# Attention over both heads of a pair at once, with the values held as the stationary operand

## The chip, the cores and the metric

One core of a Trainium2 chip runs the whole program. The metric is the device time of one execution in microseconds (us). Before the change the median of three runs is 4628.94 us (4620.43 to 4631.04). The execution that the profiler recorded took 4612.46 us, of which the profile's span is 4611.2 us.

## The reference

Two transformer blocks of depth 2 run one after the other, in float32, on 512 tokens of width 1024 (the first block has 256 context tokens beside them). Three of their four mixers' layers contain attention with heads of 64 features:

```
# block 1, both layers: 8 query heads, 2 key/value heads, each shared by 4 query heads
k_all = concat([kc, kx]); v_all = concat([vc, vx])          # 256 + 512 = 768 keys
s = einsum('bkgqd,bksd->bkgqs', q, k) * HEAD_DIM ** -0.5
p = softmax(s);  out = einsum('bkgqs,bksd->bkgqd', p, v)
# layer 0 also computes the 256 context queries against the 256 context keys
# block 2, layer 0: 8 heads with keys and values of their own, 512 tokens; every earlier block
# of 256 is selected, so it is causal attention
```

Queries and keys get an RMS norm and an axial rotation in block 1, a partial rotation in block 2. The rest, which the change does not touch, is projections, a Fourier mixer, a gated linear scan (hgrn), feed-forward layers, a short convolution and a linear recurrence (lru).

## The kernel before

Activations lie by features: 128 features on the partitions, tokens along the free dimension. One such chunk of 128 query features is a **pair** of heads, so there are four pairs, c = 0 to 3. Attention runs in three stages: `at0` (layer 0 of block 1), `at1` (layer 1) and `mo` (block 2). Each engine has its own program, written out by hand in the functions `te_` (TensorE), `ac_` (ScalarE), `ve_` (VectorE) and `gp_` (GpSimd); they meet only at semaphores (`wait_ge`; `A.up`, `V.up`, `T.up`, `G.up` raise them). `wait_bank(k)` makes TensorE wait for whoever last read bank k of PSUM; `bank(k, ...)` names that reader. Each engine works strictly in its own program's order.

**A step** is one tile of 128 queries against one head (`attend_steps`, L813). A tile is (first query, first key, number of keys, mask). `at0` has four tiles of 768 keys and two of 256 in each pair, `at1` four of 768, `mo` tiles of 128, 256, 384 and 512 keys with a causal mask on the last 128. Keys are stored once for each head, with the other head's 64 rows zeroed (`KK`, L1100, by a multiplication with the head mask `HM` on VectorE; `KZ`, L1744, the same on GpSimd), so that the full 128 rows of queries can be contracted. A step is:

- scores: queries stationary, masked keys moving, into banks 2k and 2k+1 with k = step mod 2 (L834);
- VectorE: maximum (L952), times minus the scale (L954); ScalarE: exponential with the row sum (L905);
- TensorE transposes the probabilities by blocks of 128 keys into banks 4 and 5 (L848); ScalarE copies bank 4 (L915), VectorE bank 5 (L963), and VectorE takes the reciprocal of the sum (L968);
- values: the transposed probabilities stationary, 128 columns of V moving (64 of them are of use), result by queries in bank 6 (L862);
- VectorE scales 64 columns by the reciprocal (L980); after the second head the 128 by 128 result is transposed back (L870) and ScalarE copies it into `U` (L919).

All programs are staggered two steps deep (loops at L873, L921, L983): scores of step x+2, transposes of x+1, values of x. Scores alternate between two sets of banks. The loop runs anew for each pair, so that it empties at a pair's end.

**Beside the steps** the next pair's queries are prepared, in segments at fixed steps (`AxialQueries`, L997; `PartialQueries`, L1700): square (ScalarE), head mean on TensorE (L761) and square root on ScalarE (L769), reciprocals (L773) and scaling (L777) on VectorE, rotation matmul (L783), its sine and cosine parts (L791, L794, L796). The head mean and the rotation use banks 6 and 7. GpSimd copies the finished queries `QN` to `QR` (L1054, L1742) once the last scores of the pair before are done. In `mo`, `lru` work runs beside the steps as well, with two matmuls a pair in banks 6 and 7 (L1810).

All attention matmuls are float32; the trace has two records, each a weight load and a matmul, for each of them, and one record for each transpose.

Of the kernel before, what the change touches and what calls it, by code (L numbers as in the profile page):

```python
# [12 lines left out]
P = 128  # L13
# [98 lines left out]
def program(nc, xT, cvec, cols, panels, ada_panels, w_four, lru_gates, mats, rope1, rope2, dft_x, dft_c, masks,  # L112
# [62 lines left out]
    for l in range(DEPTH):  # L175
# [15 lines left out]
        b["KK"] = [[shelf.take(f"KK{kv}{h}_{l}", [P, TOK]) for h in range(2)] for kv in range(2)]  # L191
        b["kr"] = shelf.take(f"kr_{l}", [P, TOK])
# [37 lines left out]
    for l in range(DEPTH):  # L230
# [14 lines left out]
        if l == 0:  # L245
            shelf = Shelf(top)
            b["tab"] = shelf.take("rope2_t", [P, 2, SEQ])
            b["cm"] = shelf.take("cm", [P, P])
            b["KR"] = shelf.take("KR2", [P, SEQ])
            b["KZ"] = [shelf.take(f"KZ{h}", [P, SEQ]) for h in range(2)]  # L250
# [12 lines left out]
    def emit(te, ac, ve, gp, sp):  # L263
# [492 lines left out]
        def te_head_mean(name, N):  # L756
            te.wait_ge(*A[(name, "hsq")])
            wait_bank(6)
            wait_bank(7)
            for a in range(0, N, BANK):  # L760
                t = te.matmul(PS[:, 6 + a // BANK, 0:min(N, a + BANK) - a], BO, SQ[0][:, a:min(N, a + BANK)],  # L761
                              start=True, stop=True)
            T.up(t, (name, "hms"))
            bank(6, A, name, "hrt")
            bank(7, A, name, "hrt")
# [33 lines left out]

        def te_turned(name, src, n):  # L800
# [12 lines left out]
        def attend_steps(tiles):  # L813
            return [(q0, k0, nk, dm, h) for q0, k0, nk, dm in tiles for h in range(2)]

        def te_attend(name, b, tiles, K, Vt, kv_ready, prep, other=None):
            steps = attend_steps(tiles)
            n = len(steps)
            for s in range(prep.segments):
                prep.te(0, s)  # L820
            for c in range(4):
                key = (name, c)

                def scores(x):
                    q0, k0, nk, dm, h = steps[x]
                    k = x % 2
                    if x == 0:
                        te.wait_ge(*G[key + ("QR",)])
                        if c == 0:
                            kv_ready(te)  # L830
                    wait_bank(2 * k)
                    wait_bank(2 * k + 1)
                    for a in range(0, nk, BANK):
                        t = te.matmul(PS[:, 2 * k + a // BANK, 0:min(BANK, nk - a)], b["QR"][:, q0:q0 + P],  # L834
                                      K(c, h, k0 + a, min(BANK, nk - a)), start=True, stop=True)
                    T.up(t, key + ("S", x))
                    bank(2 * k, A, name, c, "exp", x)
                    bank(2 * k + 1, A, name, c, "exp", x)

                def turn(x):  # L840
                    q0, k0, nk, dm, h = steps[x]
                    nkt, low = nk // P, nk // P // 2
                    te.wait_ge(*A[key + ("exp", x)])
                    wait_bank(4)
                    wait_bank(5)
                    for kt in range(nkt):
                        to = PS[:, 4, kt * P:(kt + 1) * P] if kt < low else PS[:, 5, (kt - low) * P:(kt - low + 1) * P]
                        t = te.transpose(to, b["PB"][x % 2][:, kt * P:(kt + 1) * P], EYE)  # L848
                        if kt == low - 1:
                            T.up(t, key + ("PTa", x))  # L850
                            bank(4, A, name, c, "PTa", x)
                    T.up(t, key + ("PTb", x))
                    bank(5, V, name, c, "PTb", x)

                def values(x):
                    q0, k0, nk, dm, h = steps[x]
                    if nk > P:
                        te.wait_ge(*A[key + ("PTa", x)])
                    te.wait_ge(*V[key + ("PTb", x)])
                    wait_bank(6)  # L860
                    for kt in range(nk // P):
                        t = te.matmul(PS[:, 6, 0:P], b["PT"][x % 2][:, kt * P:(kt + 1) * P], Vt(c, k0 // P + kt),  # L862
                                      start=kt == 0, stop=kt == nk // P - 1)
                    T.up(t, key + ("O", x))
                    bank(6, V, name, c, "OT", x)

                def turn_back(x):
                    te.wait_ge(*V[key + ("OT", x)])
                    wait_bank(7)
                    T.up(te.transpose(PS[:, 7, 0:P], b["OT"][(x // 2) % 2][:, :], EYE), key + ("back", x))  # L870
                    bank(7, A, name, c, "back", x)

                for x in range(-2, n):  # L873
                    if other:
                        other(c, x + 2)
                    if 0 <= x < prep.segments and c + 1 < 4:
                        prep.te(c + 1, x)
                    if x + 2 < n:
                        scores(x + 2)
                    if 0 <= x + 1 < n:  # L880
                        turn(x + 1)
                    if x >= 1 and steps[x - 1][4] == 1:
                        turn_back(x - 1)
                    if x >= 0:
                        values(x)
                turn_back(n - 1)

        def ac_attend(name, b, tiles, dest, prep, other=None):
            steps = attend_steps(tiles)
            n = len(steps)  # L890
            for s in range(prep.segments):
                prep.ac(0, s)
            for c in range(4):
                key = (name, c)

                def exps(x):
                    q0, k0, nk, dm, h = steps[x]
                    k = x % 2
                    ac.wait_ge(*V[key + ("nmax", x)])
                    if x >= 2:  # L900
                        ac.wait_ge(*T[key + ("PTb", x - 2)])
                        ac.wait_ge(*V[key + ("rinv", x - 2)])
                    elif c:
                        ac.wait_ge(*V[(name, c - 1, "OT", n - 2 + x)])
                    A.up(ac.activation(b["PB"][k][:, 0:nk], flat(2 * k, nk), ACT.Exp, bias=b["nmax"][k][:],  # L905
                                       scale=SCALE, accum_out=b["rsum"][k][:]), key + ("exp", x))

                def turn(x):
                    q0, k0, nk, dm, h = steps[x]
                    half = nk // P // 2 * P  # L910
                    if half:
                        ac.wait_ge(*T[key + ("PTa", x)])
                        if x >= 2:
                            ac.wait_ge(*T[key + ("O", x - 2)])
                        A.up(ac.activation(b["PT"][x % 2][:, 0:half], PS[:, 4, 0:half], ACT.Copy), key + ("PTa", x))  # L915

                def turn_back(x):
                    ac.wait_ge(*T[key + ("back", x)])
                    A.up(ac.activation(dest(c, steps[x][0]), PS[:, 7, 0:P], ACT.Copy), key + ("back", x))  # L919

                for x in range(-2, n):  # L921
                    if other:
                        other(c, x + 2)
                    if 0 <= x < prep.segments and c + 1 < 4:
                        prep.ac(c + 1, x)
                    if x + 2 < n:
                        exps(x + 2)
                    if 0 <= x + 1 < n:
                        turn(x + 1)
                    if x >= 1 and steps[x - 1][4] == 1:  # L930
                        turn_back(x - 1)
                turn_back(n - 1)

        def ve_attend(name, b, tiles, v_half, mask, prep, other=None):
            steps = attend_steps(tiles)
            n = len(steps)
            for s in range(prep.segments):
                prep.ve(0, s)
            for c in range(4):
                key = (name, c)  # L940

                def maxima(x):
                    q0, k0, nk, dm, h = steps[x]
                    k = x % 2
                    S = flat(2 * k, nk)
                    ve.wait_ge(*T[key + ("S", x)])
                    if dm:
                        V.up(ve.tensor_tensor(S[:, nk - P:nk], S[:, nk - P:nk], mask, ALU.add))
                        ve.wait_ge(*V.now())
# [1234 lines left out]
```

## Time and profile before

| quantity | value |
|---|---|
| median of 3 runs | 4628.94 us |
| profiled execution (span) | 4612.46 us (4611.2 us) |
| PE busy | 4006.7 us, 87% |
| DVE busy | 2124.5 us, 46% |
| ACT busy | 1339.6 us, 29% |
| attention steps of at0, 362 to 529 us | 167 us |
| attention steps of at1, 1688 to 1825 us | 137 us |
| attention steps of mo, 3003 to 3150 us | 147 us |

PE is the matmul side of TensorE, PEld its weight loads, DVE VectorE, ACT ScalarE, POOL GpSimd. Times in the trace count from the span's start. "Idle before, releaser" tells how long an engine stood still ahead of an instruction and which instruction ended the wait. PEclk is the clock that TensorE was granted, as a part of full speed (2.4 GHz). Matmuls overlap in time: a group's cadence, the distance of its start to the next group's start, is shorter than its printed duration.

### The profile page before, as it was taken

What the parts mean: (1) busy time and instruction counts of PE and PEld (TensorE: products, weight loads), DVE (VectorE), ACT (ScalarE), POOL (GpSimd) and SP (SyncE); (2) the same over time, 40 slices, a digit from 0 to 9 for tenths busy, and PEclk for the clock granted to TensorE, in tenths of its full rate; (3) what the DMA queues carried; (4) which work ended last, traced back from release to release, by engine and by line L of the source; (5) the groups of instructions that cost most, each with busy time, mean ns of one, the idle gap of its engine ahead of it and who ended that gap; (6) DMA issues with size and microseconds to landing.
All of it is one profiled execution on the core that took longest, in us unless ns stands there. A gap on an engine that the chain in (4) does not pass through costs nothing.

```text
span 4611.2 us, 45961 instructions
## 1 busy us (share of the span) xinstructions
PE 4006.7 (87%) x18748; PEld 3232.0 (70%) x18748; DVE 2124.5 (46%) x3323; ACT 1339.6 (29%) x1796; POOL 211.2 (5%) x324
## 2 busy tenths in 40 slices
PE   7987655899998967469998999967999899898998
PEld 6855444788887845357886886735888688676886
DVE  6536666564624246654334334265333433444334
ACT  2114433311112225333223223344222322323222
POOL 0000132000000000210000000000000000000000
PEclk8889877999998989679999999978999999999999
DMA  4310000132411210002222222201222222221222
GB/s 190 137 69 1 9 0 1 73 119 105 152 64 55 73 41 9 0 28 83 100 93 82 95 97 83 98 4 37 92 100 101 73 101 92 82 92 64 101 94 80
DMA packets 47743, 342.31 MB, mean 74 GB/s; under 512 B 5376, under 2 KB 5376, under 8 KB 7728
## 3 DMA queue, kind: packets, MB, share of 16 engines
q1 hardware_dynamic: 37728, 275.80, 16.6%
q0 software_dynamic: 8768, 61.49, 3.6%
q8 instruction: 150, 2.46, 0.2%
q10 hardware_dynamic: 1040, 2.10, 0.1%
q14 instruction: 57, 0.47, 0.0%
HBM read 337.26 MB, written 2.10 MB: 74 GB/s over the span
## 4 chain that ended last, share of the span: by engine, by line
PE 79%; DVE 11%; ACT 5%; POOL 3%; issue 2%; DMA 0%; ACTq 0%; DVEq 0%; POOLq 0%
PE PS L333 59%; PE PS L335 6%; PE PS L1166 3%; PE PS L862 2%; PE PS L834 2%; DVE SQ L425 2%; POOL E L1142 1%; DVE RS L773 1%; PE PS L374 1%; PE PS L783 1%; PE PS L848 1%; ACT WZ L1263 1%; POOL E L1143 1%; PE PS L721 1%; PE PS L393 1%
## 5 line engine op out<-in xcount | busy, mean ns | idle before, releaser
L310 DVE TENSOR_TENSOR WL<-raw,WH 128x2048 fp32r<-128x2048 f32 x260 | 595.9, 2292 | 434.6 <-ACT WH L305 434.6
L305 ACT ACTIVATE WH<-raw 128x2048 fp32r<-128x2048 f32 x260 | 495.4, 1906 | 462.7 <-PE PS L333 346.6
L1166 PE MATMUL PS<-WZ,E 128*128 128x256 f32 x560 | 165.9, 459 | 183.2 <-ACT WZ L1263 169.1
L333 PE MATMUL PS<-XH_ff,WH 128*128 128x512 f32 x704 | 280.7, 399 | 12.3 <-DVE XL_ff L436 12.3
L333 PE MATMUL PS<-XH_b,WH 128*128 128x512 f32 x704 | 277.0, 394 | 11.7 <-DVE XL_b L436 10.3
L333 PE MATMUL PS<-XH_a,WH 128*128 128x512 f32 x704 | 277.0, 393 | 11.6 <-DVE XL_a L436 10.2
L1166 PEld LDWEIGHTS PS<-WZ,E 128*128 128x128 f32 x560 | 125.7, 232 | 221.6 <-ACT WZ L1263 186.1
L333 PE MATMUL PS<-XH_ff,WL 128*128 128x512 f32 x704 | 277.2, 394 | 0.0
L333 PE MATMUL PS<-XL_ff,WH 128*128 128x512 f32 x704 | 277.1, 394 | 0.0
L333 PE MATMUL PS<-XH_a,WL 128*128 128x512 f32 x704 | 275.4, 391 | 0.0
L333 PE MATMUL PS<-XL_a,WH 128*128 128x512 f32 x704 | 275.3, 391 | 0.0
L333 PE MATMUL PS<-XL_b,WH 128*128 128x512 f32 x704 | 275.3, 391 | 0.0
L333 PE MATMUL PS<-XH_b,WL 128*128 128x512 f32 x704 | 275.1, 391 | 0.0
L333 PEld LDWEIGHTS PS<-XH_ff,WH 128*128 128x128 f32 x704 | 132.9, 189 | 46.6 <-DVE XL_ff L436 10.1
L333 PEld LDWEIGHTS PS<-XH_b,WH 128*128 128x128 f32 x704 | 132.9, 189 | 45.3 <-DVE XL_b L436 7.4
L333 PEld LDWEIGHTS PS<-XH_a,WH 128*128 128x128 f32 x704 | 132.9, 189 | 45.1 <-DVE XL_a L436 7.3
L1367 DVE COPY_PREDICATED att<-MK,PS 128x512 f32<-128x512 uint8 x140 | 102.4, 732 | 132.6 <-PE PS L1166 122.5
L333 PEld LDWEIGHTS PS<-XH_ff,WL 128*128 128x128 f32 x704 | 132.8, 189 | 29.4
L333 PEld LDWEIGHTS PS<-XL_ff,WH 128*128 128x128 f32 x704 | 133.0, 189 | 28.9
L333 PEld LDWEIGHTS PS<-XH_b,WL 128*128 128x128 f32 x704 | 133.0, 189 | 27.8
L333 PEld LDWEIGHTS PS<-XH_a,WL 128*128 128x128 f32 x704 | 133.0, 189 | 27.8
L1509 DVE TENSOR_TENSOR GA_ff<-PS,GA_ff 128x512 f32<-128x512 f32 x66 | 37.7, 599 | 248.4 <-PE PS L335 129.7
(345 smaller groups left out, 8757.6 us busy)
## 6 DMA issues: line engine op xcount, KB each, us to landing
raw<-in_panels SPq DMA_DIRECT2D x260, 1024.0 KB, 4.7
ada_ff<-in_ada_panels POOLq DMA_DIRECT2D x24, 1024.0 KB, 5.0
ada_win<-in_ada_panels POOLq DMA_DIRECT2D x16, 1024.0 KB, 5.0
ada_start<-in_ada_panels POOLq DMA_DIRECT2D x8, 1024.0 KB, 24.4
FX<-in_dft_x POOLq DMA_DIRECT2D x2, 2048.0 KB, 8.1
X<-in_xT SPq DMA_DIRECT2D x1, 3072.0 KB, 10.9
out<-X ACTq DMA_DIRECT2D x1, 2048.0 KB, 7.0
WZ<-in_masks POOLq DMA_DIRECT2D x2, 896.0 KB, 5.0
```

What stands on the lines that cost most here:

```text
L305: H.up(ac.activation(WH[s].rearrange("p k n -> p (k n)"), raw[:, s, :], ACT.Copy), n)
L310: L.up(ve.tensor_tensor(WL[s].rearrange("p k n -> p (k n)"), raw[:, s, :], WH[s].bitcast(F32).rearrange("p k n -> p (k n)"), ALU.subtract), n)
L333: t = te.matmul(PS[:, j, :], lhsT, x[:, k, 0:SEQ], start=st, stop=end)
L335: t = te.matmul(PS[:, 2 + j, 0:CTX], lhsT, x[:, k, SEQ:TOK], start=st, stop=end)
L374: t = te.matmul(PS[:, 6 + q, 0:b - a], ONES, SQ[c % 2][:, a:b], start=c == 0, stop=c == NC - 1)
L393: t = te.matmul(PS[:, 6 + j // 4, (j % 4) * P:(j % 4 + 1) * P], RC[:, j:j + 1].broadcast_to([P, P]), EYE, start=True, stop=True)
L425: t = ve.scalar_tensor_tensor(SQ[c % 2][:, a:b], X[:, c, a:b], gain(c, q), RS[:, a:b], ALU.mult, ALU.mult)
L721: t = te.matmul(PS[:, fc, 0:n], b["AB"][:, a // P + x // 2, fc, x % 2, :], b[tab][:, x % 2, x // 2, :], start=x == 0, stop=x == 2 * nt - 1)
L834: t = te.matmul(PS[:, 2 * k + a // BANK, 0:min(BANK, nk - a)], b["QR"][:, q0:q0 + P], K(c, h, k0 + a, min(BANK, nk - a)), start=True, stop ...
L862: t = te.matmul(PS[:, 6, 0:P], b["PT"][x % 2][:, kt * P:(kt + 1) * P], Vt(c, k0 // P + kt), start=kt == 0, stop=kt == nk // P - 1)
L1166: t = te.matmul(PS[:, k, fc * 2 * P:(fc + 1) * 2 * P], b["E"][d][:, lv, fc, :], b["WZ"][d][:, lv - g0, fc].rearrange("p h n -> p (h n)"), ...
L1367: V.up(ve.copy_predicated(b["att"][d][:], MK[:, d, lv, :].unsqueeze(1).broadcast_to([P, 4, P]), PS[:, 2 * d + lv % 2, :].rearrange("p (a n ...
```

## The change

A unit of work is now a **tile with both heads** (g = 0 to 4n-1, running through all four pairs without a break), where it was a step with one.

- Keys are no longer masked: `KK[kv]` and `KZ` hold both heads' 64 rows. The score matmuls contract 64 rows, `QR[rows(h)]` against `K[rows(h)]`, the two heads one after the other in each block of 512 keys. Both heads' scores fill banks 0 to 3, so that no second set is left.
- The values' matmuls have 64 columns of V stationary and the transposed probabilities moving (128 columns). Head h writes partitions 64h to 64h+63 of bank 6 + g mod 2; the two heads alternate in each block of 128 keys. The result lies by features, and the transposition back is gone.
- The reciprocals of the sums (one instruction for both heads) are spread over partitions by two more matmuls a tile: the reciprocals broadcast as 64 stationary columns, the identity moving, into columns 128 to 255 of the same bank. ScalarE copies them to `RB` ("inverses"), and VectorE multiplies the result with `RB` into `U` ("out").
- Orders change as the diff shows. The head mean names its two banks singly.
- In `gp_moba` one copy of `KR` to `KZ` takes the place of two masked products; in `ve_attention1` the four masked products are gone and the rotation writes `KK` directly.

```diff
-        b["KK"] = [[shelf.take(f"KK{kv}{h}_{l}", [P, TOK]) for h in range(2)] for kv in range(2)]
-        b["kr"] = shelf.take(f"kr_{l}", [P, TOK])
+        b["KK"] = [shelf.take(f"KK{kv}_{l}", [P, TOK]) for kv in range(2)]
...
+        def rows(h):
+            return slice(h * HD, (h + 1) * HD)
 te_attend:
+            def beside(g, s):
+                c, t = divmod(g, n)
+                if other:
+                    other(c, 2 * t + s)
+                if 2 * t + s < prep.segments and c + 1 < 4:
+                    prep.te(c + 1, 2 * t + s)
+            def scores(g):
+                c, t = divmod(g, n)
+                q0, k0, nk, dm = tiles[t]
+                if t == 0:
+                    te.wait_ge(*G[(name, c, "QR")])
...
+                for k in range(4):
+                    wait_bank(k)
+                for a in range(0, nk, BANK):
+                    for h in range(2):
+                        m = te.matmul(PS[:, 2 * h + a // BANK, 0:min(BANK, nk - a)], b["QR"][rows(h), q0:q0 + P],
+                                      K(c, h, k0 + a, min(BANK, nk - a)), start=True, stop=True)
+                T.up(m, (name, "S", g))
...
+            def values(g):
...
+                wait_bank(to)
+                for kt in range(nk // P):
+                    for h in range(2):
+                        te.matmul(PS[rows(h), to, 0:P], Vt(c, h, k0 // P + kt), b["PT"][h][:, kt * P:(kt + 1) * P],
+                                  start=kt == 0, stop=kt == nk // P - 1, skip_group_check=True)
+                te.wait_ge(*V[(name, "rinv", g)])
+                for h in range(2):
+                    m = te.matmul(PS[rows(h), to, P:2 * P], b["rinv"][:, h:h + 1].broadcast_to([P, HD]), EYE,
+                                  start=True, stop=True, skip_group_check=True)
+                T.up(m, (name, "O", g))
+                bank(to, V, name, "out", g)
+            scores(0)
+            for g in range(4 * n):
+                beside(g, 0)
+                if g:
+                    values(g - 1)
+                turn(g, 0)
+                if g + 1 < 4 * n:
+                    scores(g + 1)
+                beside(g, 1)
+                turn(g, 1)
+            values(4 * n - 1)
 ac_attend (exps waits for the maximum, for PTb of g-1 and for rinv of g-1):
+            for g in range(4 * n):
+                beside(g, 0)
+                if g:
+                    inverses(g - 1)
+                turn(g, 0)
+                turn(g, 1)
+                if g + 1 < 4 * n:
+                    exps(g + 1, 0)
+                    exps(g + 1, 1)
+                beside(g, 1)
+            inverses(4 * n - 1)
 ve_attend:
+            def out(g):
+                c, t = divmod(g, n)
+                to = 6 + g % 2
+                ve.wait_ge(*A[(name, "inverses", g)])
+                V.up(ve.tensor_tensor(dest(c, tiles[t][0]), PS[:, to, 0:P], b["RB"][:], ALU.mult), (name, "out", g))
+            for g in range(4 * n):
+                beside(g, 0)
+                if g:
+                    out(g - 1)
+                turn(g, 0)
+                if g + 1 < 4 * n:
+                    maxima(g + 1, 0)
+                    maxima(g + 1, 1)
+                turn(g, 1)
+                inverse(g)
+                beside(g, 1)
+            out(4 * n - 1)
...
-                for h in range(2):
-                    t = ve.tensor_scalar(b["KK"][kv][h][:], b["kr"][:], HM[:, h:h + 1], None, ALU.mult)
-                V.up(t, (name, "KK", kv))
...
-                for h in range(2):
-                    t = gp.tensor_tensor(b["KZ"][h][:], b["KR"][:], HM[:, h:h + 1].broadcast_to([P, SEQ]), ALU.mult)
-                G.up(t, ("mo", c, "QR"))
+                G.up(gp.tensor_copy(b["KZ"][:], b["KR"][:]), ("mo", c, "QR"))
```

## Rows read from the trace of the kernel before

**Rows 1.** The page: what the chain that ended last consists of, by engine.

```profile
PE 79%; DVE 11%; ACT 5%; POOL 3%; issue 2%; DMA 0%; ACTq 0%; DVEq 0%; POOLq 0%
```

**Rows 2.** Busy time in stretches: start:end, length, then each engine, PEclk, DMA.

```profile
362.00:529.00 167.00, 146.00 (x881) 111.68 (x881) 105.16 (x261) 73.44 (x181) 2.76 (x4) 0.97 0.00 1
1688.00:1825.00 137.00, 120.13 (x734) 92.62 (x734) 79.63 (x179) 59.13 (x125) 2.27 (x4) 0.98 0.00 1
3003.00:3150.00 147.00, 90.00 (x350) 56.21 (x350) 96.69 (x264) 70.53 (x154) 11.58 (x12) 0.79 0.00 1
```

**Rows 3.** The chain of waits in at1, last pair: start, us, what.

```profile
1801.74 1.29 PE PS L834 x4
1803.04 0.66 PE PS L848 x6
1803.69 1.34 PE PS L862 x12
...
1808.43 1.29 PE PS L834 x4
```

**Rows 4.** Timeline of the same steps: start, us, engine, line, operation.

```profile
1802.87 0.82 PE L848 MATMUL PS<-M,PB_a 128*128 128x128 f32 x6
...
1803.07 0.96 DVE L952 TENSOR_REDUCE nmax_a<-PS 128x1 f32<-128x768 f32 x1 [1.01 <-PE PS L834]
...
1804.14 0.56 DVE L963 COPY PT_a<-PS 128x384 f32<-128x384 f32 x1
```

**Rows 5.** Timeline of TensorE in ff0: matmuls of one column, and the next.

```profile
1254.77 0.99 PE L513 MATMUL PS<-one,AD_ff 128*128 128x1 f32 x8
1255.62 0.48 PE L333 MATMUL PS<-HH_ff,WH 128*128 128x512 f32 x1
```

**Rows 6.** The chain of waits in at0: small steps, a pair's start, the next, the end.

```profile
403.57 0.41 PE PS L848 x2
...
404.78 0.41 PE PS L848 x2
...
451.20 1.31 PE PS L834 x4
...
493.08 1.31 PE PS L834 x4
...
527.09 0.70 PE PS L862 x4
```

**Rows 7.** The same in at1: first scores of the second and fourth pair, and the end.

```profile
1725.36 1.31 PE PS L834 x4
...
1794.02 1.31 PE PS L834 x4
...
1821.86 1.59 PE PS L862 x12
```

**Rows 8.** Timeline of ScalarE in at0 around the square root of the preparation.

```profile
459.53 1.28 ACT L769 ACT_TABLE_LOAD   x1
...
460.91 0.90 ACT L769 ACTIVATE RS<-PS,eps 128x768 f32<-128x768 f32 x1
```

**Rows 9.** The chain of waits in at1: the preparation on VectorE and the rotation.

```profile
1679.41 3.38 DVE RS L773 x2
1682.81 0.76 DVE qn L777
...
1711.61 1.10 PE PS L783 x2
```

**Rows 10.** The chain of waits: masked keys in at1 and in mo.

```profile
1671.16 1.16 DVE KK L1100 x2
...
3008.09 2.90 POOL KZ L1744 x2
```

**Rows 11.** The same in mo: VectorE starts the lru work of the second and fourth pair.

```profile
3044.95 0.47 DVE lru_x L1819
...
3116.65 0.47 DVE lru_x L1819
```

More of the change, by code:

```diff
@@ L249, in program @@
             b["KR"] = shelf.take("KR2", [P, SEQ])
-            b["KZ"] = [shelf.take(f"KZ{h}", [P, SEQ]) for h in range(2)]
+            b["KZ"] = shelf.take("KZ", [P, SEQ])
             b["VT"] = shelf.take("VT2", [P, SEQ // P, 4 * P])
@@ L819, in te_attend @@
             for s in range(prep.segments):
                 prep.te(0, s)
[L821 to L886, printed above, removed]
@@ L891, in ac_attend @@
             for s in range(prep.segments):
                 prep.ac(0, s)
[L893 to L932, printed above, removed]
@@ L934, in ve_attend @@
-        def ve_attend(name, b, tiles, v_half, mask, prep, other=None):
-            steps = attend_steps(tiles)
-            n = len(steps)
+            exps(0, 0)
+            exps(0, 1)
+            for g in range(4 * n):
+                beside(g, 0)
+                if g:
+                    inverses(g - 1)
[5 more added lines that the diff above has]
+                beside(g, 1)
@@ new lines, in ac_attend, with ve_attend, beside, maxima @@
+            inverses(4 * n - 1)
+        def ve_attend(name, b, tiles, dest, mask, prep, other=None):
+            n = len(tiles)
+            def beside(g, s):
+                c, t = divmod(g, n)
+                if other:
+                    other(c, 2 * t + s)
+                if 2 * t + s < prep.segments and c + 1 < 4:
+                    prep.ve(c + 1, 2 * t + s)
+            def maxima(g, h):
+                q0, k0, nk, dm = tiles[g % n]
+                S = flat(2 * h, nk)
+                ve.wait_ge(*T[(name, "S", g)])
+                if dm:
+                    V.up(ve.tensor_tensor(S[:, nk - P:nk], S[:, nk - P:nk], mask, ALU.add))
+                    ve.wait_ge(*V.now())
+                if g:
+                    ve.wait_ge(*A[(name, "exp", g - 1, h)])
+                V.up(ve.tensor_reduce(b["nmax"][h][:], S, AX_X, ALU.max))
+                ve.wait_ge(*V.now())
+                V.up(ve.tensor_scalar(b["nmax"][h][:], b["nmax"][h][:], -SCALE, None, ALU.mult),
+                     (name, "nmax", g, h))
+            def turn(g, h):
+                q0, k0, nk, dm = tiles[g % n]
+                half = nk // P // 2 * P
+                ve.wait_ge(*T[(name, "PTb", g, h)])
+                if g:
+                    ve.wait_ge(*T[(name, "O", g - 1)])
+                V.up(ve.tensor_copy(b["PT"][h][:, half:nk], PS[:, 5, 0:nk - half]), (name, "PTb", g, h))
+            def inverse(g):
+                ve.wait_ge(*A[(name, "exp", g, 1)])
+                V.up(ve.reciprocal(b["rinv"][:], b["rsum"][:]), (name, "rinv", g))
+            def out(g):
+                c, t = divmod(g, n)
+                to = 6 + g % 2
+                ve.wait_ge(*A[(name, "inverses", g)])
+                V.up(ve.tensor_tensor(dest(c, tiles[t][0]), PS[:, to, 0:P], b["RB"][:], ALU.mult), (name, "out", g))
@@ L1048, in gp_attention1 @@
             table_landed.up(gp.dma_start(b["tab"][:], rope1), name)
-            n = 2 * len(attention1_tiles(l))
+            n = len(attention1_tiles(l))
             for c in range(4):
```

157 lines of the change are left out of this document (76 added, 81 removed).

## The prediction

> **What bounds the kernel now.** I read the shares of the chain of waits first: the reader is to see that TensorE holds 79% of it [rows 1]. Next, the busy times by stretch. The three attention stages take 167, 137 and 147 us, 451 of 4611.2 us, and only they can move. In at0 and at1 TensorE is busy 87% and 88% of the time at a granted clock of 0.97 and 0.98; in mo it is busy 61% at 0.79, and VectorE 66% [rows 2]. Then the chain of one undisturbed step: scores 1.29 us, six transposes 0.66, twelve records of values 1.34, and the next step's scores at once. Two steps, one tile with both heads, take 1808.43 - 1801.74 = 6.69 us, the transposition back included [rows 3]. Maxima, exponentials and copies hide behind TensorE because the stagger is two steps deep. So TensorE's work bounds a step, and what the change removes there counts only while TensorE stays the bound. Last, the turns between pairs: the third pair of at0 takes 41.9 us [rows 6], the second and third of at1 68.66/2 = 34.3 each, while the last pair of at1, which prepares nothing, needs 1821.86 + 1.59 - 1794.02 = 29.4 us for four tiles of 6.69 = 26.8 [rows 7]. Emptying and refilling costs up to 2.6 us a pair, preparation 4.9.
>
> **What TensorE does for a tile after the change.** The transposes stay (2 x 0.66). The scores have as many records and columns as before. So have the values: 24 records with 128 moving columns. The broadcasts add 4 records of 128 columns, at 1.34/12 = 0.11 us each; one transposition of 0.11 goes. Nothing becomes cheaper unless the two heads overlap in the array. They use different halves of it (64 rows each in the scores, 64 columns each in the values). No row before shows a matmul with less than the full array, so I bound it. Without overlap scores are 2.58, values 2.68 + 0.45 = 3.13. With full overlap they cost what one head costs: 1.29, and 1.34 + 0.22 = 1.56 [rows 3]. The two records of one head cannot overlap each other, and if matmuls begin in program order (A1 A2 B1 B2), the best is one slot of lag: scores 1.72, values 13 slots + 3 slots = 1.78. A further limit would be what one record costs to issue: eight records with one column each take 1255.62 - 1254.77 = 0.85 us, 0.106 each, as much as 128 columns do [rows 5]. Those loads are 128 columns wide, the new ones 64, so the row does not say whether the load or the issue holds it.
>
> **The new cycle.** This is the step that decides. The second set of score banks is gone, and values(g) wait for VectorE's copy of the second head, which stands on VectorE behind both maxima of tile g+1, which wait for scores(g+1). From the end of scores(g+1): 0.20 to the first maximum, 2 x 1.07 for the maxima with their scaling (1803.07 to 1804.14), 0.56 for the copy [rows 4], 0.06 to start: 2.96 us, in which TensorE has only 0.66 us of transposes to do. Then values(g), transposes(g+1, first head) and scores(g+2). A tile of 768 keys takes 2.96 + V + 0.66 + S:
>
> - full overlap: 2.96 + 1.56 + 0.66 + 1.29 = 6.47
> - one slot of lag: 2.96 + 1.78 + 0.66 + 1.72 = 7.12
> - no overlap: 2.96 + 3.13 + 0.66 + 2.58 = 9.33
>
> Against 6.69 now. So the overlap of the heads, if it happens, only pays for the pipeline that is lost. I take 6.8, between the first two, since nothing in the rows chooses between them. The exponentials are not on this cycle: they start some 3.0 us after the scores' end and the first is ready 1.05 later, when the values run. A tile of 256 keys by the same sum takes 3.3 to 4.0 us (I take 3.4) where two steps now take 2 x 1.21 = 2.4 (404.78 - 403.57) [rows 6].
>
> **What is saved and added around it.** The loop no longer empties at a pair's end; QR is copied a tile ahead, so GpSimd is hidden. Preparation now hurts in two places. The head mean writes bank 6, which values(g) of the same tile needs, and ScalarE takes the root after both exponentials: exponentials end at 4.8 us, table load 1.28, root 0.70 (0.90 in at0) [rows 8]; values start at 6.85 instead of 2.96, +3.9. In at1 the rotation stands ahead of values on TensorE and waits for a reciprocal and the scaling on VectorE (3.38/2 + 0.76 after 2.96), and takes 1.10 itself [rows 9]: +3.5. In at0 I get +0.85 (reciprocals delay the next maxima) and +1.0 (values wait for the sine) for it.
>
> at1: the start to the end of scores(1) about 7.8, 14 tiles x 6.8 = 95.2, preparation 3 x 7.4 = 22.2, tail 3.8: 129.0, against 1823.4 - 1688 = 135.4 [rows 2, 7]: -6.4. The masked keys' 1.16 are on the chain and go [rows 10]: -7.6. (The start is scores at a low clock, 2.7, then 3.5 to the second exponential's end, and the next scores.)
>
> at0: 7.8 + 15 x 6.8 + 8 x 3.4 + 3 x 5.95 + 2 = 156.9, against 527.8 - 362 = 165.8 [rows 2, 6]: -8.9. Its masked products lie beside matmuls and transposes of V; they gain nothing.
>
> mo: a pair lasts 71.7/2 = 35.9 us [rows 11]. The same sum over its four tiles gives 18 us, to which the lru work adds what it does now (gate matmuls that wait for sigmoids in the value banks, 3; square root and gelu with their table loads ahead of ScalarE's copies, 4; VectorE's 12 us of lru and rotation, of which perhaps 8 don't fit into the gaps): 33. With three turns -9; the masked product before the first scores shrinks from 2.90 to a copy of about 0.6 [rows 10], -2.3; -12 with the rest.
>
> Sum -28. To this a cost per change between array shapes, which no row shows: six transposes are printed with 0.82 us but step on after 0.66 [rows 3, 4], so letting one group finish before the next begins costs up to 0.16, and two such changes lie on each tile's cycle (values to transposes, transposes to scores): 56 tiles x 2 x 0.16 = 18 us at most, 0 at least; I take 8. Result **-20 us**: 4592 us for the profiled execution of 4612.46. The median of the runs shown lies 16.5 us above that execution, so I predict 4628.94 - 20 = **4609 us**.
>
> The Trainium skill, "TensorEngine Tiling (Array Packing)", section Key Properties, speaks against the change: changing the tiling mode drains TensorE. It gives no price; by it the whole 18 us would be due and the sum -10. The trace before cannot show it, having one mode only. The same section has different tiles work in parallel, by which full overlap would hold: the cycle 6.47 and the sum near -36. No run so far shows it.
>
> **Rivals.**
>
> *No overlap of the heads* (0.26). For it: two records per float32 matmul and a cadence that rows show only as serial. Against it: different halves of the array and different banks or partitions. The place is scores and values in every tile, the price 9.33 - 6.8 = 2.5 us for each of 29 tiles of 768 keys beyond the start, 0.6 for the small ones, some 13 in mo, 4 for starts and tails: +93, so -20 + 93 = +73: **4702**. It decides from a cycle of about 7.5 us on: 0.7 x 29 eats up the 20.
>
> *Only the scores overlap* (0.14): the values are held by issue or loads at 0.11 a record [rows 5]. +1.4 x 29 + 4 + 7 = +53 on -20: +33, **4662**.
>
> *The clock falls* (0.10). TensorE idles 2.3 us of each 6.8 and longer where the root holds it. mo has a clock of 0.79 with TensorE busy 61% [rows 2]; were at0 and at1 to come to 0.80, the 3.8 us of matmuls on each cycle would take 0.95 longer: 31 x 0.95 = +30, so +10: **4639**. Against it: no idle stretch of a plain tile is long.
>
> *Forecast* (0.50): overlap, own range 4585 to 4634 (full overlap with no cost of shapes and a better mo, to lag with the whole 18).
>
> **Chances.** A measurement tells about 0.2% here, 9 us. Of the forecast's 0.50, 0.38 lies more than 9 us below, 0.09 within, 0.03 above; the clock gives 0.02 faster, 0.03 same, 0.05 slower; the other two are slower. Faster 0.40, same 0.12, slower 0.48. The range is 4585 to 4705: it leaves out a twentieth below, and above only an unoverlapped case with dear changes of shape.
>
> **What would show it.** In the changed trace: score starts of undisturbed tiles of at1 6.4 to 7.2 us apart (over 9: no overlap); TensorE idle some 2.3 us ahead of the values with VectorE's copy as releaser; the values' 24 records in 1.4 to 1.5 us; a wait of values for the root (L769) of some 4 us once a pair; no emptying between pairs. I am wrong if the values start right behind the second transposes, or if mo, worked out most roughly, moves by more than 20 us.

## The result: slower by 0.7%

The changed kernel takes 4658.28 us (median of 6 runs, 4647.6 to 4670.46), the kernel before, measured beside it, 4627.91 (6 runs). The ratio is 1.0067, 95% interval 1.0048 to 1.0086. I forecast 20 us less and got about 30 more. The profiled execution took 4649.52 us (span 4647.6), 37.1 more than before.

The stages of the changed kernel, from the first copy of QR to the last output; columns as in [rows 2]:

```profile
364.20:539.80 175.60, 119.00 (x952) 82.09 (x952) 97.12 (x213) 75.85 (x180) 3.28 (x4) 0.89 0.00 1
1702.30:1863.50 161.20, 104.22 (x780) 71.95 (x780) 75.00 (x146) 60.84 (x124) 2.45 (x4) 0.83 0.00 1
3041.80:3185.60 143.80, 86.63 (x396) 47.46 (x396) 87.61 (x226) 69.86 (x152) 4.67 (x8) 0.63 0.00 1
```

The kernel before, cut where VectorE's last scaling ends (the last transposition back and its copy, which the change removes, take 0.7 us more in each stage):

```profile
361.40:528.10 166.70, 145.66 (x879) 111.51 (x879) 105.16 (x261) 73.09 (x179) 3.31 (x4) 0.97 0.00 1
1687.80:1823.80 136.00, 119.46 (x731) 92.28 (x731) 79.46 (x178) 58.76 (x123) 2.46 (x4) 0.98 0.00 1
3007.20:3148.30 141.10, 87.63 (x347) 55.58 (x347) 93.38 (x258) 68.91 (x150) 11.58 (x12) 0.79 0.00 1
```

With these 0.7 us, at0 is 8.2 us longer, at1 24.5 and mo 2.0: together 35 of the 37 us of the profile. TensorE is busy *less* in all three stages (at1: 104 us instead of 119) and the stages are longer. It waits more, and its granted clock went from 0.98 to 0.83 in at1.

A plain tile of 768 keys after the change; it answers to [rows 3, 4]. The bracket is the idle time before a group and its releaser. TensorE:

```profile
1835.93 1.56 PE L835 MATMUL PS<-KK,QR_a 64*128 64x512 f32 x8
1837.42 0.88 PE L849 MATMUL PS<-M,PB_a 128*128 128x128 f32 x6
1840.49 1.60 PE L867 MATMUL PS<-PT_a,VT 128*64 128x128 f32 x24 [2.19 <-DVE rinv_a L974]
```

VectorE, with the first maximum of the tile before:

```profile
1830.50 0.96 DVE L959 TENSOR_REDUCE nmax_a<-PS 128x1 f32<-128x768 f32 x1 [0.94 <-PE PS L835]
...
1837.54 0.96 DVE L959 TENSOR_REDUCE nmax_a<-PS 128x1 f32<-128x768 f32 x1 [0.94 <-PE PS L835]
...
1839.68 0.56 DVE L970 COPY PT_a<-PS 128x384 f32<-128x384 f32 x1
1840.16 0.15 DVE L974 RECIPROCAL rinv_a<-rsum_a 128x2 f32<-128x2 f32 x1
```

The mechanism is the forecast one. Eight score records of both heads take 1.49 us, where four took 1.29 [rows 3]; 24 records of values take 1.34 (1840.49 to the broadcasts at 1841.83), as twelve did. TensorE then waits 2.19 us with VectorE as releaser. The cycle is 7.04 us (1830.50 to 1837.54; forecast 6.8, before 6.69).

The two tiles of a pair that carry the preparation, at1:

```profile
1797.00 0.82 PE L849 MATMUL PS<-M,PB_a 128*128 128x128 f32 x6
1803.06 2.83 PE L867 MATMUL PS<-PT_a,VT 128*64 128x128 f32 x24 [5.24 <-ACT RS L766]
1805.64 0.67 PE L871 MATMUL PS<-M,rinv_a 128*64 128x128 f32 x4
1806.24 1.54 PE L849 MATMUL PS<-M,PB_a 128*128 128x128 f32 x6
...
1814.59 2.07 PE L780 MATMUL PS<-qn,M 128*128 128x512 f32 x2 [4.50 <-DVE qn L774]
1817.61 2.83 PE L867 MATMUL PS<-PT_a,VT 128*64 128x128 f32 x24 [0.94 <-DVE QN_a L788]
```

The values wait 5.24 us for the root. Then the same 24 records take 2.83 us instead of 1.53, the broadcasts 0.67, the transposes 1.54 instead of 0.87, at a granted clock that is down to 1.2 of 2.4 GHz at first (0.53 from 1803 to 1808 us; in the plain tile it is 1.00 from 1838 to 1841.8). The maxima of these tiles start 13.2 and 14.1 us before the next ones. I had 10.7 and 10.3.

### The profile page after: what moved, and what is told of

Its sections match the earlier page's. It is cut to its first block, busy times and chain, and to the rows that moved or that the text cites. A ratio compares the mean times of both kernels' runs of the same rounds, so it can differ in the third digit from the quotient of the medians.

```text
span 4647.6 us, 46103 instructions
## 1 busy us (share of the span) xinstructions
PE 3965.9 (85%) x18916; PEld 3175.2 (68%) x18916; DVE 2101.4 (45%) x3203; ACT 1344.2 (29%) x1796; POOL 204.0 (4%) x320
## 4 chain that ended last, share of the span: by engine, by line
PE 78%; DVE 11%; ACT 5%; POOL 3%; issue 2%; DMA 1%; ACTq 0%; DVEq 0%; POOLq 0%
PE PS L332 58%; PE PS L334 5%; PE PS L1165 3%; PE PS L835 2%; PE PS L867 2%; DVE SQ L424 2%; POOL E L1141 1%; DVE nmax_a L959 1%; PE PS L849 1%; PE PS L780 1%; ACT WZ L1262 1%; POOL E L1142 1%; DVE YS L1602 1%; PE PS L720 1%; PE PS L373 1%
## 5 line engine op out<-in xcount | busy, mean ns | idle before, releaser
L332 PEld LDWEIGHTS PS<-XL_b,WH 128*128 128x128 f32 x704 | 133.2, 189 | 26.9
## 6 DMA issues: line engine op xcount, KB each, us to landing
ada_start<-in_ada_panels POOLq DMA_DIRECT2D x8, 1024.0 KB, 24.5
```

What stands on the lines that cost most here:

```text
L332: t = te.matmul(PS[:, j, :], lhsT, x[:, k, 0:SEQ], start=st, stop=end)
```

## The experiments

Ratios are to the kernel before, measured beside each run. Lengths of stages are read from the one profiled execution of a kernel; stages of the kernel before are cut as above, 0.7 us short. The theory at the start: the lost 30 us are preparation, which now holds TensorE, and its clock. The rivals: heads that don't overlap, or the price of shapes.

### Preparation left out, before and after

```diff
 def te(self, c, s):          # likewise ac and ve, in AxialQueries
+    if c:
+        return
```

> The kernel before, with the preparation of the queries of pairs 1 to 3 left out in at0 and at1 (the queries of pair 0 are used again, so this part of the computation is missing). In the trace before, a pair of at1 takes 34.3 us with preparation and 29.4 without, one of at0 42 to 43.6 and about 35. Every theory expects 3 x 4.9 + 3 x 8 = 39 us less, about 0.9915 of before. It is the base for the next kernel.

> The changed kernel with the same part left out. Theory P (the loss comes from where the preparation makes TensorE wait in the new order, and from the low clock after these waits): at1 becomes 7.8 + 14 x 7.04 + 4 = 110 us instead of 161, at0 loses some 18 us, together -68 from the changed kernel, so that it ends within 10 us of the kernel before without preparation. Rival Q (the plain tile or another part of the change costs the time): it loses the same 39 us as the kernel before does and stays some 30 us above that one.

Measured: 4579.08 us (0.9915, 0.9898 to 0.9931) and 4601.52 (0.9965, 0.9952 to 0.9978). Stages before: at0 144.8, at1 123.2, mo 141.6. After:

```profile
364.50:521.10 156.60, 108.39 (x928) 75.17 (x928) 71.59 (x192) 63.95 (x168) 3.28 (x4) 0.91 0.00 1
1688.50:1812.60 124.10, 85.73 (x768) 60.95 (x768) 56.89 (x128) 49.87 (x112) 2.44 (x4) 0.92 0.00 1
```

So in at1 the new attention by itself is level (124.1 to 123.9, with the 0.7 us), and preparation costs 37.1 us there instead of 12.8. In at0 preparation costs 19.0 instead of 21.9: at0's 8 us come from the tiles, which take 11 more.

Neither expectation holds as a whole. P wanted the changed kernel to end within 10 us of the other, Q 30 above it; it ends 22 above. Of these 22, 11 are at0's tiles, 2 are mo, and 9 lie between at0 and at1, in work that the change doesn't touch. This stretch takes 1159 us in both kernels before, 1162 in the changed one and 1167 here, and 1177 in the run of the rotation's marks below. No run explains that. It is why a mended stage can be plain in the profile and not in the whole time.

### Heads one after the other

```diff
-for kt in range(nk // P):
-    for h in range(2):
+for h in range(2):
+    for kt in range(nk // P):        # the same for the scores
```

> The changed kernel with the two heads' matmuls in another order only: all of head 0, then all of head 1, in scores and in values. Theory O (heads overlap in the array because their matmuls alternate): without alternation scores of a tile of 768 keys take about 2.6 us instead of 1.5, values about 2.7 instead of 1.5, a plain tile 9.3 instead of 7.04, and the kernel gets 32 x 2.3 + 12 = about 85 us slower than the changed one, 1.025 of before or more. Rival: the 64-wide operands are cheaper by themselves, or the engine overlaps them in any order; then nothing changes.

Measured: 4695.92 us, 1.0166 (1.0148 to 1.0185). TensorE, a plain tile of at1:

```profile
1874.56 0.88 PE L849 MATMUL PS<-M,PB_a 128*128 128x128 f32 x6
1877.64 2.10 PE L867 MATMUL PS<-PT_a,VT 128*64 128x128 f32 x21 [2.20 <-DVE rinv_a L974]
1879.47 0.32 PE L871 MATMUL PS<-M,rinv_a 128*64 128x128 f32 x1
1879.57 0.27 PE L867 MATMUL PS<-PT_a,VT 128*64 128x128 f32 x1
...
1881.02 1.57 PE L835 MATMUL PS<-KK,QR_a 64*128 64x512 f32 x8
1882.52 0.88 PE L849 MATMUL PS<-M,PB_a 128*128 128x128 f32 x6
```

The scores overlap even in this order (1.50), the values in part: about 2.3 us instead of 1.34, and a broadcast of one head starts before the other head's last values. The cycle is 7.96 (1874.56 to 1882.52), not 9.3. Alternating the heads is worth 0.9 us a tile here; it isn't what makes overlap possible. The whole loses 0.010 of its time against the changed kernel, some 46 us, where theory O wanted 85.

### Half rows in the kernel before

```diff
-b["QR"][:, q0:q0 + P]
+b["QR"][h * HD:(h + 1) * HD, q0:q0 + P]     # K rows likewise; masked K kept
```

> The kernel before with one thing of the change: its score matmuls contract only the 64 rows of their head (keys stay masked, steps and order stay). The heads lie in different steps, so nothing can overlap; what is left is the change of array shape, twice a step. If a change costs 0.15 us as the transposes behind the values suggest in the changed kernel (0.81 instead of 0.66), 112 steps x 2 x 0.15 = 34 us, of which some 25 on the path: 1.005. If changes of shape are free: 1.000.

Measured: 4667.75 us, 1.0104 (1.0083 to 1.0125). A step of at1, which lasts 3.63 to 3.74 us where it lasted 3.34 [rows 3]:

```profile
1855.34 1.55 PE L834 MATMUL PS<-KK,QR_a 64*128 64x512 f32 x4
```

and the stages:

```profile
364.40:555.80 191.40, 167.23 (x879) 119.57 (x879) 105.67 (x261) 73.06 (x179) 3.26 (x4) 0.88 0.00 1
1722.10:1871.60 149.50, 129.91 (x731) 93.70 (x731) 79.70 (x178) 58.74 (x123) 2.45 (x4) 0.92 0.00 1
3054.70:3205.30 150.60, 114.36 (x347) 65.38 (x347) 94.26 (x258) 69.25 (x150) 11.57 (x12) 0.65 0.00 1
```

TensorE's busy share is about the same in at0 and at1 and higher in mo (87% and 87%, 88% and 87%, 62% and 76%); its idle time grew by 3 us in each of at0 and at1. And yet the clock falls from 0.97, 0.98 and 0.79 to 0.88, 0.92 and 0.65. The loss is 48 us, twice the 25 that changes of shape alone were to cost. Half-filled matmuls cost twice: at each change of shape, and in the granted clock. Whether the clock answers to the half rows or to the changes themselves, this run doesn't part.

### The price of a change of shape

```diff
 for kt in range(nkt):
+    if kt and name == "at1":
+        r = P if g // n < 2 else HD
+        te.matmul(PS[:, 5, 3 * P:3 * P + 1], EYE[0:r, :], EYE[0:r, 0:1], ...)
```

> The changed kernel without the preparation of pairs 1 to 3 in at0 and at1 (that work is left out), and in at1 a product with one column after each of the first five of six transposes: of the full array (128 rows) in pairs 0 and 1, of 64 rows in pairs 2 and 3. The two products differ in nothing but the shape, so ten changes of shape stand in one group of transposes of pairs 2 and 3 and none in that of pairs 0 and 1. Theory A (a change of shape costs 0.15 to 0.2 us): the transposes' group takes 0.81 + 5 x 0.21 = 1.9 us in pairs 0 and 1, and 1.5 to 2.0 us more in pairs 2 and 3. Rival B (the 0.15 us longer groups of the changed kernel are the lower clock or the load of a new tile, not the change of shape): both are alike within 0.3 us.

This part of the computation is missing, and it is one execution (4692.65 us). TensorE with the full array's products, then with those of 64 rows, both at a granted clock of 1.00:

```profile
1722.76 0.28 PE L851 MATMUL PS<-M 128*128 128x1 f32 x2
1722.91 0.31 PE L852 MATMUL PS<-M,PB_a 128*128 128x128 f32 x1
1723.05 0.28 PE L851 MATMUL PS<-M 128*128 128x1 f32 x2
...
1790.85 0.38 PE L851 MATMUL PS<-M 64*128 64x1 f32 x2
1791.16 0.33 PE L852 MATMUL PS<-M,PB_a 128*128 128x128 f32 x1
1791.42 0.38 PE L851 MATMUL PS<-M 64*128 64x1 f32 x2
```

From product to product: 0.29 us without a change of shape, 0.57 with two. **One change costs 0.14 us.** At the low clock the round takes 0.91. The rival, that the trace's 0.15 was something else, falls for changes of rows; the change to and from 64 columns has no run of its own.

The clock goes down too. These two lines are pairs 0 and 1, where the added products change no shape, and the end of the stage:

```profile
1700.00:1768.00 68.00, 59.73 (x470) 48.89 (x472) 24.75 (x56) 21.91 (x49) 1.23 (x2) 0.76 0.00 1
1813.00:1890.00 77.00, 72.74 (x317) 51.44 (x316) 17.02 (x38) 15.15 (x34) 0.45 (x1) 0.50 0.00 1
```

Already the full array's one-column products bring it to 0.76, where the same 68 us of the kernel without preparation have 0.95, and TensorE is busier (60 us to 47). So this run doesn't show that changes of shape alone lower the clock: what a matmul does in the array seems to count, but what about it does stays open.

### The banks that hold TensorE

```diff
-te_head_mean(name, self.N)
+te_head_mean(name, self.N, to=7 if self.l else 6)    # and the root reads there
```

> The changed kernel with one edit in at1: the head mean is written to bank 7 instead of bank 6, and the root reads it there. Nothing of the computation is left out. Theory A (TensorE's wait for the root at tile 0 exists only because bank 6 is both the mean's and the values'): the values of tile 0 start some 2.95 us after the first maximum instead of 6.91, and, since no long idle stretch comes ahead of them, take 1.53 us instead of 2.83; that tile's cycle goes from 13.2 to about 7.1. Three pairs prepare in at1: -18 us, at1 161 to about 143, the kernel -0.4%. Rival B (the preparation's work itself, table loads, reciprocals and rotation, holds the pair, whatever the bank): the wait moves to the rotation of tile 1, which becomes longer by what tile 0 gains, and at1 stays within 5 us of 161.

Measured: 4646.06 us, 1.0046 (1.0033 to 1.0059); at1 151.0 instead of 161.2. The values of tile 0 no longer wait for the root:

```profile
1760.26 1.53 PE L868 MATMUL PS<-PT_a,VT 128*64 128x128 f32 x24 [1.29 <-DVE rinv_a L975]
...
1766.61 0.84 PE L850 MATMUL PS<-M,PB_a 128*128 128x128 f32 x6 [2.30 <-DVE PT_a L971]
1771.63 2.08 PE L781 MATMUL PS<-qn,M 128*128 128x512 f32 x2 [4.18 <-DVE qn L775]
```

Their tile takes 9.1 instead of 13.2, not 7.1: a reciprocal of the preparation (1.75 us) now stands on VectorE ahead of the copy, and the transposes wait 2.30 us for it. The wait for the rotation stays. Ten of the 18 us came, between A and B; in the whole time they aren't shown, since the interval overlaps that of the changed kernel.

```diff
-self.segments = 4 + self.pieces      # at1: rotation beside tile 1
+self.segments = 7                    # rotation beside tile 2, in bank 7
 def te_rotate(..., to=6):            # waits for and marks the banks it writes
```

> The changed kernel with at1's head mean in bank 7 as in the first kernel of this call, and besides at1's rotation in bank 7 alone and one segment later (beside tile 2 instead of tile 1), marking only the banks that it writes. Nothing is left out. Theory A (both waits of preparation on TensorE are waits for banks and for a scaling that comes a step too late): all cycles of at1 become 7.05 but for some 1 us of TensorE's own preparation, so at1 is near the 124.1 us that it has without preparation: 125 to 132, -29 to -36 us, the kernel -0.7%, which is level with the kernel before. Rival B (VectorE, ScalarE and GpSimd work of preparation is on the path of a tile anyway): at1 stays above 145. Rival C (the low clock of at1 comes from the smaller matmuls and not from the waits): the waits go, but the granted clock of at1 stays at about 0.82, and at1 ends near 140.

Measured: 4615.28 us, 0.9985 (0.9974 to 0.9995), clear of the changed kernel; at1 133.5, mo 135.5, at1's clock 0.88. That is nearly A, which wanted 125 to 132, and not C, which wanted 140 at a clock of 0.82. The rotation finds its input ready:

```profile
1764.57 1.56 PE L835 MATMUL PS<-KK,QR_a 64*128 64x512 f32 x8
1766.06 1.12 PE L780 MATMUL PS<-qn,M 128*128 128x512 f32 x2
```

That mo gained 8 us I hadn't expected (143.8 to 135.5). It needed a run of its own:

```diff
-wait_bank(6); wait_bank(7)           # te_rotate, whatever its width
+wait_bank(6 + a // BANK)             # only what is written; marks likewise
```

> The changed kernel with one edit: a rotation waits for and marks only the banks that it writes, so one of 512 columns (at1, mo) leaves bank 7 alone. Nothing is left out. Theory A (values of odd tiles in bank 7 wait for a sine that has nothing to do with them): the 7.8 us that the trace of the changed kernel has ahead of the values of mo with the sine as releaser go, with what the clock gives back: mo 144 to about 135; in at1 the 0.94 us ahead of the values behind the rotation go, 3 to 5 us in all; 4658 to about 4646, ratio 1.004. Rival B (mo is held by ScalarE's lru work, and at1's rotation tile by the scaling): mo and at1 move by less than 3 us each.

Measured: 4646.94 us, 1.0057 (1.0039 to 1.0075); mo 143.8 to 135.5, at1 157.8. The values of mo, in the changed kernel and with this one edit (busy, mean ns, then the idle time before them by releaser):

```profile
L867 PE MATMUL PS<-PT_m,VT 128*64 128x128 f32 x160 | 20.2, 410 | 31.3 <-DVE rinv_m L974 17.0 <-DVE KR L788 7.8 <-ACT lru_r L1791 3.7
```

```profile
L865 PE MATMUL PS<-PT_m,VT 128*64 128x128 f32 x160 | 19.6, 399 | 24.6 <-DVE rinv_m L972 18.1 <-ACT lru_r L1789 3.7 <-DVE QN_m L786 2.8
```

The 7.8 us behind KR, the key's sine, are gone. A rotation of 512 columns writes bank 6 and had marked bank 7, where the values of odd tiles now go. The gain is beyond what mo varies by: in the two runs that edit at1 alone it takes 147.1 us, with the marks mended 135.5 both times. In the whole kernel's time this isn't shown: the ratio's interval overlaps that of the changed kernel.

### Is it the wait or the clock?

```diff
+fill(11)      # at1, ahead of the values that wait for the root
+fill(10)      # at1, ahead of the rotation's wait; 256 columns each, unread
```

> The changed kernel with matmuls added in at1 whose results nobody reads: eleven of 256 columns ahead of the values that wait for the root, ten ahead of the rotation that waits for the scaling. Nothing of the computation is left out and no wait is removed. Theory A (about 2 us at each of these two places are the granted clock, which falls to half while TensorE idles and makes the values 2.83 instead of 1.53 and the transposes 1.47 instead of 0.81): with TensorE busy the values after the wait take about 1.6, the transposes 0.8; each pair gains 3 to 4 us, at1 161 to about 150, the kernel -0.2%, although TensorE has more to do. Rival B (the clock falls for a reason other than the idle stretch, such as matmuls of half the array): values after the wait stay at 2.83, and at1 stays or grows by the added matmuls.

Measured: 4645.28 us, 1.0044 (1.0032 to 1.0056); at1 148.6 at a clock of 0.96. After the filling:

```profile
1755.54 4.99 PE L818 MATMUL PS<-M 128*128 128x256 f32 x22 [1.29 <-DVE rinv_a L982]
1760.45 1.53 PE L875 MATMUL PS<-PT_a,VT 128*64 128x128 f32 x24
```

The root ends no earlier (6.9 us after the scores' end in both), the filling even runs 1.1 us past it, and the values take 1.53 instead of 2.83. So at least 12.6 of at1's 24.5 lost us are the clock: they came back although TensorE ran 126 records more. In the whole time this isn't shown either: the interval overlaps that of the changed kernel. The Trainium skill, "TensorE: Matmul & The Clock Gate", section "HAM oscillation — how this bites in real kernels", advises to arrange the work so that TensorE doesn't wait between its groups; the trace agrees with it, 1.53 us for these values against 2.83.

### VectorE's order

```diff
 turn(g, 0)
+inverse(g)
 maxima(g + 1, 0)
-maxima(g + 1, 1)
 turn(g, 1)
-inverse(g)
+maxima(g + 1, 1)
```

> The changed kernel with another order on VectorE: copy of head 0, reciprocal, maximum of the next tile's head 0, copy of head 1, maximum of the next tile's head 1. Before, both maxima stood ahead of the copy of head 1. Nothing is left out. Theory A (a plain tile's cycle is VectorE's way from the scores' end over both maxima and the copy, plus values, transposes and scores): one maximum of 1.07 us leaves the way, a plain tile takes 7.04 - 0.95 = about 6.1 us, and 29 tiles of at0 and at1 give 28 us: the kernel -0.6%. Rival B (the exponentials, which now wait for a later second maximum, take its place): the cycle shrinks by less than 0.4 us, the total by under 12 us. Rival C (TensorE's own work is the bound): no change at all.

Measured: 4641.78 us, 1.0036 (1.0022 to 1.005), which just meets the interval of the changed kernel; at0 168.6, at1 147.0, so 21 us in the profile where A wanted 28. A plain tile takes 5.97 us (7.04 - 1.07, one maximum to the hundredth); TensorE's wait went from 2.19 to 1.12:

```profile
1744.47 1.53 PE L867 MATMUL PS<-PT_a,VT 128*64 128x128 f32 x24 [1.12 <-DVE PT_a L970]
```

That confirms what the cycle consists of, and rivals B and C fall. The values still start 0.25 us after the copy's end, with the reciprocal no longer behind it, so the reciprocal isn't what holds them.

### Together

> The two mended things together: VectorE's copy of head 1 between the maxima, and at1's mean and rotation in bank 7, the rotation one segment later. Nothing is left out. The gains lie at different places (plain tiles 7.04 to about 6.0; preparation tiles of at1), so theory A adds them: 43 us for the banks with what mo gains, 17 for the order, about 4598 us where the changed kernel has 4658, a ratio of 0.994 to the kernel before. Rival B (preparation tiles are bound by ScalarE and VectorE, which the new order does not relieve): only plain tiles gain, and the sum is within 8 us of the kernel with the banks alone, 4615.

Measured: **4596.57 us, 0.9934 (0.992 to 0.9947)**: the gains add, as A had it (0.994). The stages:

```profile
363.20:531.80 168.60, 118.19 (x952) 82.80 (x952) 97.19 (x213) 77.09 (x180) 3.30 (x4) 0.90 0.00 1
1698.80:1823.20 124.40, 95.07 (x780) 66.29 (x780) 73.66 (x146) 60.74 (x124) 2.45 (x4) 0.88 0.00 1
3000.70:3131.70 131.00, 82.64 (x396) 44.19 (x396) 86.38 (x226) 71.44 (x152) 4.65 (x8) 0.70 0.00 1
```

> The kernel with order and banks mended, and ahead of every tile's values four (in mo five) products of 128 x 128 x 128 whose results nobody reads, in free columns of the values' own bank, while TensorE waits there for VectorE's copy. Nothing is left out. Theory A (a large part of what matmuls cost in these stages is the granted clock, 0.9 in at0 and at1 and 0.64 in mo, which TensorE's idle stretches bring down): the clock of mo rises above 0.8 and mo gets 8 to 15 us shorter, at0 and at1 2 to 6 each. Rival B (the matmuls of half the array hold the clock down): the clocks stay, and the added 0.9 us stand on the path of short tiles: slower by 5 to 15 us. Rival C (mo is bound by ScalarE and VectorE): the clock rises there and the stage's length does not move.

Measured: 4604.84 us, 0.9952 (0.994 to 0.9965). at1 gained (118.7, clock 0.93), at0 lost (172.3) and mo lost (136.2) although its clock rose to 0.79. Theory A fails in mo. Either TensorE's clock isn't what holds mo, or the 160 added records there eat up what it gives; this run doesn't part them. In at0 the filling stood behind the wait for the bank and not in front of it, so at the root it came too late and delayed the values at a low clock:

```profile
426.10 2.08 PE L862 MATMUL PS<-M 128*128 128x128 f32 x8 [4.94 <-ACT RS L767]
```

> The kernel with order and banks mended, with products whose results nobody reads in two places only: four of 128 columns ahead of each tile's values in at1, and fourteen in at0 between VectorE's copy and the wait for the root. Nothing is left out. Theory A (behind the root's wait of 5.0 us in at0, values, broadcasts and transposes take 2.83 + 0.67 + 1.54 because the clock is at half, instead of 1.53 + 0.22 + 0.81): at0 169 to about 162, at1 124 to 119 as when all tiles were filled, so 4585 us, ratio 0.991. Rival B (the fill only delays the values): at0 stays at 169 or grows, the total is 4591 to 4600.

Measured: 4587.43 us, 0.9933 (0.9913 to 0.9953); at0 160.4 at a clock of 0.95, at1 119.6. At the root's wait in at0:

```profile
419.46 3.36 PE L816 MATMUL PS<-M 128*128 128x128 f32 x28 [0.74 <-DVE PT_a L979]
423.66 1.53 PE L876 MATMUL PS<-PT_a,VT 128*64 128x128 f32 x24 [0.84 <-ACT RS L767]
```

The two stages shortened by 13 us in the profile, as theory A had it (at0 162, at1 119), but the ratio to the kernel before equals that of the unfilled version, so a gain of the whole isn't shown.

## Why the prediction was wrong

**Overlap: right.** Two heads cost one head's time in the values and 0.2 us more in the scores, and the rival without overlap (4702) is refuted. VectorE's way is the cycle, as drawn.

**The plain cycle: 7.04 instead of 6.8.** Against full overlap (6.47) it has 0.57 more: transposes 0.80 for 0.66 and broadcasts 0.35 for 0.22 (a change of shape follows each; one of rows measured 0.14 alone), scores to first maximum 0.12 more, and 0.25 instead of 0.06 from the copy's end to the values. The drain at a mode change, which the Trainium skill states in "TensorEngine Tiling (Array Packing)", section "Key Properties", and which the prediction weighed beside its sum, agrees with these rows, now with a price. I took 8 us for the changes where 18 were in view; at 0.14 they come to 16.

**Preparation in at1: the step that failed.** The forecast had 7.4 us a pair, 22.2 in all; 37.1 were measured. Both waits were sized rightly: values start 7.0 us after the scores' end (forecast 6.85), the rotation 5.4 (2.96 + 3.38/2 + 0.76 = 5.4). Missing were two things. Each of these long waits is followed by work at half clock, which costs 2.2 us behind the root and 2.7 behind the wait for the scaling (0.95 in the rotation itself, 1.76 from the values to the scores). And the sum lets the values behind the rotation start at once, while the rotation marks their bank 7, so they wait for VectorE's sine (0.94 us) with nothing beside them. I had priced the clock as a rival of its own with a chance of 0.10, "no idle stretch of a plain tile is long", and forgot the preparation's stretches that I had just worked out at 4 us each.

**at1's frame (start, cycles and tail): 17 us short.** Without preparation my sum is 106.8 and the run 124.1. The tail from the last scores' end is 10.4, not 3.8: two tiles' values come behind it, and I had counted one. The start is 9.9 for 7.8. The 14 cycles take 103.7 for 95.2: 3.4 for the plain cycle, the rest in three tiles of 8.6 at a low clock. These stand behind waits of 2.2 us like all the others, so even a plain tile, whose idle stretch is short, can run at the low clock.

**at0: the same.** Its preparation was right (19.0 measured, 17.9 forecast). Without it, its 22 cycles take 140.6 us where mine are 122.4 (the 23rd of my sum stands for part of the tail). At full clock a pair takes 35.7 for 34, since small tiles need 4.7 and 4.4, not 3.4: 7 us in four pairs. The other 11 are tiles at a low clock (7.5 to 8.6).

**mo: +2.0 instead of -12.** At least 8.3 us are the marked bank 7. I had named bank holding for at0 and at1 and not carried it to mo, where a pair has only four tiles and two rotations. The other 6 have no run of their own: mo's sum was the roughest, and its clock fell from 0.79 to 0.63.

**The whole.** Of about 32 us by which at1 missed, 15 are preparation and 17 the frame; at0 adds 17, mo 14; 8 of the sum stood in my term for the shapes. By these readings the low clock has about 12 us in at1's preparation, 5 in its cycles and 11 in at0's: 28 of 63. The rest are the tail, the marked bank, the small tiles and the plain cycle. So the rival *The clock falls*, priced at +30, had the mechanism and the size that the forecast lacked, and the other terms came on top of it.

The range (4585 to 4705) held the time; the sign was wrong. That 4658 lies beside the 4662 of *Only the scores overlap* is luck, for the values overlap too; by its own terms that rival's extra is 52 and not 53. What stays open: how much of the clock in plain stretches is the half-filled matmuls and how much the 2.19 us waits. The kernel of before with half rows shows that the first exists; none here parts them in the changed kernel.

## What to carry to other kernels

When a change halves TensorE's work, ask what its new waits do to its clock: the work behind the preparation's waits of 5.2 and 4.5 us ran at half speed here, so they cost about half again their length. List every bank that each helper waits for and marks, and not only those that it writes, whenever buffers move to other banks. And when one engine's serial way becomes the cycle, try its order first: moving one copy ahead of one maximum took 1.07 us off each tile here, and with the banks mended as well, the changed kernel is 0.7% faster than the kernel before instead of 0.7% slower.

## What was not expected of the hardware

Matmuls on different halves of the array overlap even if a whole head is issued ahead of the other (eight score records in 1.50 us), and in the values a record of one half starts before earlier ones of the other half. A change between 128 and 64 rows costs 0.14 us at the high clock. And matmuls of 64 rows, with the changes of shape around them, brought the granted clock down (0.98 to 0.92 in at1 with TensorE busy 88% and 87%, 0.79 to 0.65 in mo with it busy 62% and 76%). Full-array products of one column did so too (0.95 to 0.76).
